# Moving TensorE's wait for the small token bank into the slab, and spreading one norm over more turns, in a three-block float32 kernel

## The reference

```python
h_res = jnp.concatenate([meta, x], axis=1)             # 16 + 1024 tokens
proj = rmsnorm(h_res, norm_g[l]) @ w_in[l]             # first block's slabs
...
y_b = gated_short_conv(bg, cg, xh, conv_w[l])          # second block: bg * conv(cg * xh)
mixed = jnp.concatenate([y_a, y_b, y_c], axis=-1)
mixed = rms_norm(mixed.reshape(b, s, N_GROUPS, 64), g).reshape(b, s, MIX_WIDTH)
x = x + jnp.einsum('bse,ed->bsd', mixed, w_out[l])
```

## Time and profile before

| what | us |
|---|---|
| median of 3 executions | 3727.33 (3724.28 to 3728.81) |
| the profiled execution | 3724.08 |
| its span in the trace | 3722.8 |
| PE busy in the span | 3644.1 |
| DVE, ACT, POOL busy | 1756.8, 1153.8, 1094.2 |

### The profile page before, as it was taken

The page is one execution under the profiler, slowest core; times in us unless marked ns, Lnnn a source line. Parts: engine busy times, 40 slices in busy tenths (PEclk is TensorE's granted clock), DMA queues, the critical chain, the costliest instruction groups (busy, mean ns, idle before and its releaser), DMA issues.

```text
span 3722.8 us, 42438 instructions
## 1 busy us (share of the span) xinstructions
PE 3644.1 (98%) x17740; PEld 3003.8 (81%) x17740; DVE 1756.8 (47%) x2289; ACT 1153.8 (31%) x1491; POOL 1094.2 (29%) x747
## 2 busy tenths in 40 slices
PE   7999999999999999999999999999999999999998
PEld 6999987888888877887888888877777778888886
DVE  6676616999553473344422222227566642222226
ACT  5555522221241344443321111124322332112113
POOL 4343421222233441112522222225113432222223
PEclk9999999999999999999999999999999999999999
DMA  2100021111242340012211111114112221111112
GB/s 104 35 29 29 23 91 46 52 57 57 74 147 91 105 147 30 31 36 68 96 51 49 48 46 47 50 51 133 35 35 74 68 68 46 46 51 46 46 51 74
DMA packets 65134, 229.31 MB, mean 62 GB/s; under 512 B 7216, under 2 KB 7472, under 8 KB 64944
## 3 DMA queue, kind: packets, MB, share of 16 engines
q1 hardware_dynamic: 64944, 226.60, 18.5%
HBM read 201.40 MB, written 25.17 MB: 61 GB/s over the span
## 4 chain that ended last, share of the span: by engine, by line
PE 89%; DVE 7%; issue 2%; ACT 1%; POOL 0%; DMA 0%; SPq 0%; DVEq 0%; ACTq 0%
PE psum L521 79%; PE psum L644 2%; PE psum L913 1%; PE psum L880 1%; PE psum L895 1%; PE psum L615 1%; DVE fb L2156 0%; PE psum L768 0%; PE psum L730 0%; PE psum L668 0%; PE psum L667 0%; DVE hl L2087 0%; DVE pb L2946 0%; DVE Ab L2191 0%; DVE k L2912 0%
## 5 line engine op out<-in xcount | busy, mean ns | idle before, releaser
L3204 POOL TENSOR_TENSOR wl<-raw,wh 128x512 fp32r<-128x512 f32 x636 | 884.3, 1411 | 2317.9 <-ACT wh L1225 2317.9
L521 PE MATMUL psum<-hh,wh 128*128 128x512 f32 (+2 forms) x3760 | 1203.0, 391 | 30.0 <-POOL wl L3204 9.1
L521 PE MATMUL psum<-hh,wl 128*128 128x512 f32 (+2 forms) x3760 | 1162.9, 380 | 0.0
L521 PE MATMUL psum<-hl,wh 128*128 128x512 f32 (+2 forms) x3760 | 1159.7, 379 | 0.0
L521 PEld LDWEIGHTS psum<-hh,wh 128*128 128x128 f32 x3760 | 679.4, 189 | 183.4 <-issue 35.5
L521 PEld LDWEIGHTS psum<-hl,wh 128*128 128x128 f32 x3760 | 695.7, 189 | 132.4
L521 PEld LDWEIGHTS psum<-hh,wl 128*128 128x128 f32 x3760 | 696.5, 189 | 127.4
L1225 ACT ACTIVATE wh<-raw 128x1024 fp32r<-128x1024 f32 x318 | 335.2, 1054 | 773.1 <-PE psum L521 769.8
L521 PE MATMUL psum<-hdh,wh 128*128 128x512 f32 x1024 | 333.7, 398 | 5.0 <-DVE B L3105 4.4
L521 PE MATMUL psum<-hdl,wh 128*128 128x512 f32 x1024 | 330.9, 396 | 0.0
L521 PE MATMUL psum<-hdh,wl 128*128 128x512 f32 x1024 | 330.8, 395 | 0.0
(11 more groups left out here) (436 smaller groups left out, 2950.6 us busy)
## 6 DMA issues: line engine op xcount, KB each, us to landing
raw<-in_wts SPq DMA_DIRECT2D x318, 512.0 KB, 3.5
keep_x<-B SPq DMA_DIRECT2D x14, 512.0 KB, 5.9
X<-in_xin SPq DMA_DIRECT2D x8, 520.0 KB, 5.2
keep_sz<-tmp SPq DMA_DIRECT2D x8, 512.0 KB, 2.9
tmp<-keep_sz SPq DMA_DIRECT2D x8, 512.0 KB, 4.0
av<-keep_gr SPq DMA_DIRECT2D x8, 512.0 KB, 3.3
av<-keep_gc SPq DMA_DIRECT2D x8, 512.0 KB, 3.7
xc<-keep_x SPq DMA_DIRECT2D x8, 512.0 KB, 5.3
```

What stands on the lines that cost most here:

```text
L521: ins = pe.matmul(out, w, x[:, k, c0:c0 + width], start=first and n == 0, stop=final and n == 2)
L3204: gp.tensor_tensor(wl[:, s, a], raw[:, s, a], fp(wh[:, s, a]), SUB).then_inc(*c.lo.tick(i, p))
```

## The change

It has two parts. In `gemm` the head's wait is no longer put where the bank is taken: the bank and the wait are handed to `three`, which issues the wait between the groups `parts` and `lead` of the first tile. The order of the products is the same. In `group_norm` a number `late` is added, 6 for tile 0 of the short convolution and 0 for all others: three turns pass before the norm takes its banks, and eleven instead of five between the sums and the rows. The programs of the other engines stay as they are.

```diff
-        def three(pr, hd, i, k, kw, first, final, xh, xl, off, halves=(0, 1)):
+        def three(pr, hd, i, k, kw, first, final, xh, xl, off, halves=(0, 1), lead_free=None):
...
-            for g in groups:
+            for z, g in enumerate(groups):
+                if z and lead_free:
+                    pe.wait_ge(*lead_free)
                 for n, (w, x) in enumerate(((a, xh), (b, xh), (a, xl))):
...
-            hd = grab(head, (i,), lead) if lead else None
+            hd, lead_free = head.take((i,), lead) if lead else (None, None)
...
-                ins = three(pr, hd, i, k, k, n == 0, n == KT - 1, hh, hl, META)
+                ins = three(pr, hd, i, k, k, n == 0, n == KT - 1, hh, hl, META, lead_free=lead_free)
...
-        def group_norm(ks):
+        def group_norm(ks, late=0):
+
+            yield from pause(late // 2)
             xs = [grab(aux, ("gs", ks[0], g), c.gn_act("root", ks[0], g)) for g in range(2)]
...
-            for _ in range(5):
-                yield
+            yield from pause(5 + late)
...
-            yield from group_norm([m])
+            yield from group_norm([m], 0 if m else 6)
```

## The result

The changed kernel takes 3708.65 us (median of 4 runs, 3703.85 to 3709.70) beside 3725.81 for the kernel before, measured with it (4 runs, 3723.24 to 3728.81): 17.2 us less, a ratio of 0.9949 with an interval from 0.9936 to 0.9961. The forecast was 3708.1. Measured a second time it was 3706.60 (4 runs) beside 3727.48 (14 runs), 20.9 us less (0.9948, 0.9931 to 0.9964). Both intervals lie wholly under 1, so the gain of about 0.5% is clear of the scatter. The profiled execution is one of 3709.7 us.

What follows compares the result with a forecast made beforehand. PE was taken to bound the kernel, busy 3644.1 of 3722.8 us. The moved wait's 12.3 and the later norm's 6.9 sum to 19.2 us, taking the median from 3727.3 to 3708.1, range 3703 to 3716.

Steps and rivals of the forecast that it cites:

- The cost of a joint: Where two slabs with a head bank follow each other, PE loses 0.90 us: 0.66 idle, 0.24 overlap and restart.
- the dead heat: At typical joints six products cover the head's wait to 0.01 us: load due at 678.51, gate opens at 678.52.
- restart of 0.24: Rival: head's gate slightly late, PE restarts at each of thirteen joints, 3.1 us less gain, 3711.2; chance 0.15.
- 107 ns for a weight load: Estimated 128-column load held by a late gate; exposed at thirteen joints it would take 1.4 us from the sum.
- The new wait behind the recurrence's joints: Before `turned_v`, behind tile 0 of f, 0.18 us is taken back: six joints give 4.3 us.
- The two long joints: At 576 and 69 us ACT is late; the wait stays but shrinks, gaining 0.95 and 0.75 us.
- part one: The head's wait moved behind six products at the fifteen joints: 12.3 us gained, bounds 9.2 and 13.5.
- No other engine binds: DVE keeps 2.9 us free per 47.24 us convolution period; rival that another engine binds, 3720.4, chance 0.04.
- Part two: Later norm in slab SHORT + 3: three waits and the half clock go, 22.19 to 15.3 us, 6.9 gained.
- the clock falls anyway: Rival: the norm's 8-row products load PE little, half clock falls on full products, up to 3.4 us back, 3711.5; chance 0.09.
- The sum: Whole kernel: 12.3 + 6.9 = 19.2 us gained, median 3727.3 to 3708.1, profiled execution 3724.1 to 3704.9.
- half-clock stretches elsewhere: Sign of being wrong: half-clock stretches coming up in other places of the new profile; no size given.

Runs made afterwards that it cites:

- part_one: Kernel before with only the head's wait moved, tile 0's norm keeping its turns: 3714.39 us beside 3727.48, ratio 0.9966.
- sums_late: Changed kernel with only the delay ahead of the norm's sums, five turns again between sums and rows: one execution, span 3708.8 us, slab SHORT + 3 21.2.
- rows_late: Changed kernel with only the delay ahead of the norm's rows, the sums in the second turn as before: one execution, span 3708.3 us, slab SHORT + 3 17.0.
- The parts' medians: Kernel before with the moved wait alone, 3714.39 us, and with the later norm alone, 3719.46 us, both beside 3727.48.

## Why the prediction was right, step by step

**The cost of a joint and the dead heat: right.** In the convolution branch the head's first products of two neighbouring slabs start at 624.44 and 671.68, a period of 47.24, as worked out. From 427 to 1409 us the lead grows by 12.43 - 5.18 = 7.25 us; seven joints of 0.90 and the long one of 0.95 are 7.25. Nothing of the restart of 0.24 remained, so that rival is out. The prediction's 107 ns for a weight load was low, since the loads of these products last 0.19 us in the trace; at thirteen joints that would have been 2.5 us, and none of it came. The rule of the Trainium skill ("TensorE: Matmul & The Clock Gate", Part 2, "Step-by-step") that loads run ahead of products agrees with the load at 123.30, 0.16 ahead of its product, behind a gate that had opened in time.

**The new wait behind the recurrence's joints: mechanism right, size off.** Forecast was 0.18 us at each head and a period shorter by 0.72. Matching transposes and products stand at 163.30 and 217.14 before (53.84) and 162.37 and 215.39 after (53.02), 0.82 shorter, so the new wait takes 0.08, and the profile shows no idle time of PE for it. The weight load does start late, at 123.92, 0.04 behind ACT's end (123.88). But its product starts at 123.94, 0.17 behind the last product into the head (123.77), its usual distance. I had taken the load's delay for the product's; a load that is ahead by a step has that step to lose. This term is 6 x 0.1 = 0.6 us better than the sum had it.

**The two long joints: one right, one given back.** At 576 and 69 us I expected idle times of 0.6 to 0.9, and they are 0.36 and 0.29. The forecast mixed two counts here: 1.32 or 1.54 plus the restart of 0.24, less 0.95, is the whole loss left (0.6 and 0.8), of which the profile shows a part as idle time; counted in steps of 0.158 the traces have about 0.6 at both. The 0.95 at 576 is all gained (the 7.25 above). The one at 69 us should have given 0.75, and gives about 0.1. The cause is a wait that I didn't foresee. PE's timeline there, after:

```profile
69.76 0.43 PE L524 MATMUL psum<-hh,wh 128*128 128x348 f32 x1 [0.29 <-ACT vb L1400]
...
70.40 1.09 PE L638 MATMUL psum<-cst,vb 128*128 128x128 f32 x8
...
73.90 0.66 PE L654 MATMUL psum<-cst,work 128*128 128x128 f32 x4 [0.53 <-ACT vb L1332]
74.32 0.72 PE L524 MATMUL psum<-hh,wh 128*128 128x346 f32 x3
```

The transposes of v start at 70.40 where they started at 71.29. Behind tile 1 come those of k, into the banks that ACT empties at line 1332, and at head 0 ACT is late with that, since it still has the decays' exponentials and the next `wh` to make (it copies at 73.25, and did at 73.24 before). PE waits 0.53 for it, and the products behind start at 74.32, where they started at 74.42. I followed PE's queue by one step, to `turned_v`, and not by two. The two misses, +0.6 and -0.6, cancel by luck: part one was forecast at 12.3, and the first stretch is 12.4 to 12.6 shorter.

**No other engine binds: right.** DVE's busy time in 47 us of the convolution branch is 44.07, and PE is busy for all 47.00.

**Part two: right.** 15.1 us against a forecast of 15.3, clock 1.00, no idle time; 7.1 gained (forecast 6.9). That the gain is more than the 4.23 of the waits shown goes with the clock: 0.66 and 0.69 in part_one and sums_late behind the waits, 1.00 in rows_late without them; the 2.4 us for it in the prediction weren't measured apart. The rival "the clock falls anyway" is out for this slab. The rule of the Trainium skill, "TensorE: Matmul & The Clock Gate", Part 1, "What's actually happening", half or all of the pulses by how busy PE has lately been, agrees with these three: 0.66 and 0.69 behind the idle time, 1.00 without it.

**The sum.** At SHORT + 4 the lead is 19.5 us, and first stretch and slab together are 19.5 shorter (12.4 + 7.1); forecast 19.2. In time it was 17.2 and 20.9 less, 19.0 on the mean. That the median of 3708.65 came within 0.6 us of the 3708.1 is partly luck: the kernel before came out at 3725.81, 1.5 under the 3727.33 that the forecast started from, and the gain was 2.0 under the 19.2. For the profiled execution the forecast was 3704.9, and it took 3709.7. The parts' medians (13.1 and 8.0) are each a little above their stretches (12.6 and 7.1), so the medians show no loss in the rest.

**What I had no step for** is that rest. I listed half-clock stretches elsewhere as a sign of being wrong. They did come up, and the profiled execution gave back 5 us beside the trace of before. The changed kernel profiled again gave back none, so the change doesn't bring them by itself; whether it brings a little more of them on the mean isn't shown. The scatter that I allowed for at the lower end, 3 us, came from this without my knowing it. Why one execution's clock falls at 2850 and another's, behind the same wait of 1.8 us, does not, is open: the rows show the wait and the granted clock and nothing that differs. What a half clock costs is less open: it is less where PE waits for DVE behind it.

## What to carry to other kernels

A wait for a buffer belongs at the first instruction that writes that buffer, with as much independent work ahead of it as the releaser is late; here six products (0.95 us) were just enough, three left about 0.4 us at each joint, and a wait that is met cost nothing that could be measured. When a stall goes, follow the queue behind it two instructions far, not one: at head 0 the next wait but one took the gain back. And where the clock falls behind waits, the loss is larger than the waits shown (7.1 us against 4.23). But judge small edits by their own stretch of the trace, since the clock elsewhere moves a single execution by up to 6 us.

## What the runs showed of the hardware

- Half-clock stretches in the last 2000 us move between executions of one program: rest of 2022.1 and 2015.8 us for the changed kernel, with the same work and, up to SHORT + 4, the same waits. At the same place, ahead of a wait for DVE, a half clock shortened the wait (0.37 for 1.95 us) and cost nothing there.
- The same four products behind the same wait took 1.98 us in one trace and 2.98 in another.
- Waits that are already met cost nothing measurable: 248 of them changed a stretch of 1630 us by less than 0.1.
- A weight load let through 0.15 us late (123.92, where one step ahead of its product would be 123.77), most of a product's step of 0.158, cost 0.08 us by the period.
